# A mixture-of-experts stage on one core: expert rows are gated at evacuation and added into the result table by an indirect DMA

## What is computed

```python
h = rmsnorm(x2) * g_ffn
lg = h @ w_rg + b_rg;  grp = argmax(lg);  gate1 = softmax(lg)[grp]
top_v, top_i = top_k(expert logits within grp, 2)
gates = gate1 * softmax(top_v)                   # two gates per token
y[t]  = sum over the token's two experts e of
        gates[t, e] * ((silu(h[t] @ w_g[e]) * (h[t] @ w_u[e])) @ w_d[e])
out   = rmsnorm(x2 + y) * g_final
```

## Time and profile before

| | |
|---|---|
| median of 3 runs | 2068.12 us (2067.97 to 2071.73) |
| the profiled execution's own time | 2068.49 us |
| its span, first to last instruction | 2066.7 us |
| PE busy | 1762.6 us (85%) |
| DVE busy | 509.8 us (25%) |
| ACT busy | 325.3 us (16%) |
| POOL busy | 287.2 us (14%) |
| HBM read, written | 517.52 MB, 30.91 MB |
| q1, the DMAs issued by SP | 513.81 MB, 66.0% of 16 engines' span |
| q0, the DMAs issued by POOL | 19.17 MB, 3.2% |

### The profile page before, as it was taken

One profiled execution on the slowest core, in us unless ns is written; L12 is line 12 of the kernel. 1 busy time (PEld: TensorE's weight loads), 2 busy tenths in 40 slices (PEclk: granted clock), 3 DMA queues, 4 the chain that ended last, 5 costly groups with the idle time before them and its releaser, 6 DMA issues.

```text
span 2066.7 us, 27101 instructions
## 1 busy us (share of the span) xinstructions
PE 1762.6 (85%) x10986; PEld 1238.5 (60%) x10987; DVE 509.8 (25%) x1090; ACT 325.3 (16%) x573; POOL 287.2 (14%) x225
## 2 busy tenths in 40 slices
PE   7999999999899999985887787778787888977880
PEld 6888888887578888873544444434444454544440
DVE  6410999535365200014000000000000000000006
ACT  4003111004623011111111110101010111101112
POOL 0681322215800000000000000000000000000000
PEclk9999999999999999997999999998999999999895
DMA  5264121336954223317999999999999597999995
GB/s 234 64 153 111 68 81 61 122 147 190 14 199 162 102 82 125 140 37 292 386 405 422 395 413 395 406 391 393 393 398 393 199 399 324 412 403 411 414 416 218
DMA packets 88821, 535.86 MB, mean 259 GB/s; under 512 B 28761, under 2 KB 37465, under 8 KB 43673
## 3 DMA queue, kind: packets, MB, share of 16 engines
q1 hardware_dynamic: 74528, 513.81, 66.0%
q0 software_dynamic: 8800, 19.17, 3.2%
q10 hardware_dynamic: 5440, 2.13, 0.6%
HBM read 517.52 MB, written 30.91 MB: 265 GB/s over the span
## 4 chain that ended last, share of the span: by engine, by line
PE 53%; DMA 38%; POOL 3%; DVE 3%; ACT 2%; issue 1%; SPq 0%; POOLq 0%; ACTq 0%; DVEq 0%
DMA arena<-w_up_in 36%; PE psum L533 35%; PE psum L807 11%; PE psum L823 2%; DMA arena<-y_rows 1%; PE psum L662 1%; PE psum L668 1%; PE psum L570 1%; PE psum L787 1%; DVE arena L1564 1%; PE psum L732 1%; DVE arena L1557 1%; DMA y_rows<-arena 0%; POOL arena L1040 0%; POOL arena L1043 0%
## 5 line engine op out<-in xcount | busy, mean ns | idle before, releaser
L533 PE MATMUL psum<-arena 128*128 128x260 f32 x3328 | 741.5, 386 | 18.0 <-ACT arena L845 13.1
L533 PEld LDWEIGHTS psum<-arena 128*128 128x128 f32 x3328 | 637.1, 192 | 118.5 <-issue 10.2
L807 PE MATMUL psum<-arena 128*64 128x256 f32 x4352 | 541.8, 408 | 177.3 <-DMA arena<-w_up_in 150.5
L807 PEld LDWEIGHTS psum<-arena 128*64 128x64 f32 x4352 | 331.3, 148 | 397.0 <-DMA arena<-w_up_in 174.2
L823 PE MATMUL psum<-arena 128*64 128x512 f32 x1088 | 255.0, 623 | 16.9 <-ACT arena L1003 16.1
L1550 DVE TENSOR_TENSOR arena<-arena,psum 128x256 f32<-128x256 f32 x34 | 14.3, 421 | 959.9 <-PE psum L807 959.9
L823 PEld LDWEIGHTS psum<-arena 128*64 128x64 f32 x1088 | 78.1, 143 | 171.9 <-issue 143.5
L1128 POOL DMA_INDIRECT y_rows<-arena x34 | 33.9, 996 | 986.3 <-ACT arena L1008 941.2
L1003 ACT ACTIVATE arena<-psum 128x256 f32<-128x256 f32 x34 | 13.1, 384 | 509.2 <-PE psum L813 509.2
L787 PEld LDWEIGHTS psum<-arena 64*128 64x128 f32 x560 | 64.8, 203 | 22.1 <-issue 22.1
L1008 ACT ACTIVATE arena<-psum 128x512 f32<-128x512 f32 x68 | 36.9, 594 | 261.2 <-PE psum L823 261.2
(11 more groups left out here) (294 smaller groups left out, 1076.1 us busy)
## 6 DMA issues: line engine op xcount, KB each, us to landing
arena<-w_down_in SPq DMA_DIRECT2D x64, 2048.0 KB, 26.1
arena<-w_gate_in SPq DMA_DIRECT2D x64, 2048.0 KB, 28.1
arena<-w_up_in SPq DMA_DIRECT2D x64, 2048.0 KB, 27.7
arena<-w_in_in SPq DMA_DIRECT2D x32, 1024.0 KB, 4.8
arena<-w_out_in SPq DMA_DIRECT2D x16, 1024.0 KB, 4.8
arena<-k_cache_in SPq DMA_DIRECT2D x8, 1024.0 KB, 6.8
arena<-v_cache_in SPq DMA_DIRECT2D x8, 1024.0 KB, 4.8
arena<-y_rows SPq DMA_DIRECT2D x8, 1024.0 KB, 8.1
```

Source lines behind the costliest of these rows:

```text
L533: last = mm(pair(n)[:, h, :], w(kk), rhs(kk)[:, HALF * h:HALF * (h + 1)], start=(kk == begin), stop=(kk == kn - 1 and stop))
L807: last = mm(ps[64 * h:64 * h + 64, i // 2, 0:256], xtr[:, kk, :], w[:, kk, 256 * h:256 * (h + 1)], start=(kk == 0), stop=(kk == 15))
```

## The change

The table `y_rows` gives way to `y_sum`, with two rows of 1024 values per token, which is x2's shape. `store_x2` stores each group of x2 columns a second time, into `y_sum`. The scatter adds to its destination rows (`compute_op=ALU.add`). Since it adds, the rows have to carry their gate: each block needs its 128 gates as a column (`gate_now`), which comes from a one-hot product on PE with f32 operands, made once in block 0, and ACT multiplies by it in the evacuation. The order of a token's two experts (`swap`) no longer matters, and with it fall its DVE steps, one half of the list product, and in the tail the early loads and both gated additions. The tail loads `y_sum` after the last scatter into the weights' buffers and goes on to the norm. POOL waits for the second stores of x2 (`s_yst`) after its first two gathers.

The diff, cut to its core (declarations of buffers and semaphores are left out):

```diff
@@ SP @@
             def store_x2(g):
...
                 sp.dma_start(x2_rows[SEQ:T, c], x2_of[4][0:NS, c]).then_inc(s_x2st, 16)
+                c = slice(512 * g, 512 * (g + 1))
+                sp.dma_start(sums[0:SEQ, c].rearrange("(i p) n -> p i n", p=P), x2row[:, 0:4, c]).then_inc(s_yst, 16)
+                sp.dma_start(sums[SEQ:T, c], x2_of[4][0:NS, c]).then_inc(s_yst, 16)
...
-            last_base = sp.value_load(base_i[0:1, NE - 1:NE], min_val=1, max_val=NBLK)
-            sp.wait_ge(s_sct, last_base * 16)
...
-            load_y(f_low, 0, 4, s_flow)
-            sp.wait_ge(s_gdone, more + NE)
-            for i in range(4):
-                load_y(f_low, 0, i, s_flow)
             sp.wait_ge(s_ddone, more + NE)
             sp.dma_start(fg, t["g_final"].to_broadcast([P, DM])).then_inc(s_gf, 16)
             sp.wait_ge(s_sct, more * 16 + 16 * NE)
             for i in (4, 0, 1, 2, 3):
-                load_y(f_high, 1, i, s_fhigh[i])
+                sp.dma_start(fx[i][0:TOKS[i]], sums[P * i:P * i + TOKS[i], :]).then_inc(s_frow[i], 16)
@@ PE @@
-                last = mm(ps[:, 4, 0:2 * NBLK].rearrange("p (v b) -> p v b", v=2), lo16[:, c, :], hv16[:, c],
-                          start=(c == 0), stop=(c == 9))
+                last = mm(ps[:, 4, 0:NBLK], lo16[:, c, :], hv16[:, c, :], start=(c == 0), stop=(c == 9))
...
+                if first(n):
+                    pe.wait_ge(s_gate, 1)
+                    for c in range(10):
+                        last = mm(ps[:, 7, 0:NBLK], lo32[:, c, :], gate_b[:, c, :], start=(c == 0), stop=(c == 9))
+                    last.then_inc(s_gp, 1)
                 turn_rows(n + 1)
@@ ACT @@
+                act.wait_ge(s_is, n + 1)
                 act.wait_ge(s_ddone, n + 1)
                 for b in range(2):
-                    A(yrow[:, 512 * b:512 * (b + 1)], ps[:, 5 + b, :], ACT.Copy).then_inc(s_yv, 1)
+                    A(yrow[:, 512 * b:512 * (b + 1)], ps[:, 5 + b, :], ACT.Copy, scale=gate_now[:, j:j + 1]
+                      ).then_inc(s_yv, 1)
...
-                act.wait_ge(s_fin, c + 1)
+                act.wait_ge(s_frow[i], 16)
@@ POOL @@
                 pool.indirect_dma_start(
-                    out=y_rows, out_offset=bass.IndirectOffsetOnAxis(ap=idx_now[:, 2 + j:3 + j], axis=0),
+                    out=y_sum, out_offset=bass.IndirectOffsetOnAxis(ap=idx_now[:, 2 + j:3 + j], axis=0),
                     in_=yrow, in_offset=None,
-                    bounds_check=4 * T - 1, oob_is_err=False).then_inc(s_sct, 16)
+                    bounds_check=2 * T - 1, oob_is_err=False, compute_op=ALU.add).then_inc(s_sct, 16)
...
+            pool.wait_ge(s_yst, 16 * 8)
             blocks(pool, expert)
@@ DVE @@
-            tt(hv16[:, :, 0, :], wide_b, over(id_, NBLK), ALU.mult)
-            tt(hv16[:, :, 1, :], wide_b, over(tok1, NBLK), ALU.mult).then_inc(s_hot, 1)
+            tt(hv16, wide_b, over(tok1, NBLK), ALU.mult).then_inc(s_hot, 1)
...
-            for g in (first_gate, second_gate):
-                link(tt(g[:, :, 1:2], g[:, :, 0:1], swap.unsqueeze(2), ALU.mult))
-                link(tt(g[:, :, 0:1], g[:, :, 0:1], g[:, :, 1:2], ALU.subtract))
-            tt(gate_w[:, :, 0:1], first_gate[:, :, 0:1], second_gate[:, :, 1:2], ALU.add)
-            link(tt(gate_w[:, :, 1:2], first_gate[:, :, 1:2], second_gate[:, :, 0:1], ALU.add))
+            tt(lo32, iota_s.unsqueeze(1).to_broadcast([P, 10, P]), over(w_, P), ALU.is_equal)
+            tt(gate_b, wide_b, over(gate_w, NBLK), ALU.mult).then_inc(s_gate, 1)
...
+                if first(n):
+                    dve.wait_ge(s_gp, 1)
+                    link(dve.tensor_copy(gate_of, ps[:, 7, 0:NBLK]))
+                dve.tensor_copy(idx_now[:, 2 + j:3 + j], idx_s[:, bass.ds(n, 1)])
+                dve.tensor_copy(gate_now[:, j:j + 1], gate_of[:, bass.ds(n, 1)]).then_inc(s_is, 1)
...
-            for i, n in enumerate(TOKS):
-                stt(fx[i][0:n, 0:DM], f_low[i][0:n], gate_w[0:n, i, 0:1], fx[i][0:n, 0:DM], ALU.mult, ALU.add
-                    ).then_inc(s_fadd, 1)
...
-                stt(fx[i][0:n, 0:DM], f_high[i][0:n], gate_w[0:n, i, 1:2], fx[i][0:n, 0:DM], ALU.mult, ALU.add
-                    ).then_inc(s_fin, 1)
```

More of the change, by code:

```diff
@@ L243, in build @@
         s_z0 = sem("spare_scales_zeroed")
-        s_fin, s_fq, s_frt, s_fo = sem("final_loaded"), sem("final_sumsq"), sem("final_root"), sem("final_ready")
+        s_fq, s_frt, s_fo = sem("final_sumsq"), sem("final_root"), sem("final_ready")
         s_fst = sem("final_stored")
-        s_flow = sem("low_rows_loaded")
-        s_fhigh = [sem(f"high_rows_loaded{j}") for j in range(5)]
-        s_fadd = sem("low_rows_added")
+        s_frow = [sem(f"final_rows_loaded{j}") for j in range(5)]
+        s_yst, s_gp, s_gate = sem("sums_started"), sem("slot_gates_psum"), sem("slot_gates_ready")
         s_held = sem("pool_waited")
@@ L271, in build @@
         keep = Cols(ms + 4 * XW + DM // 2)
-        gate_w = keep(10).rearrange("p (t j) -> p t j", t=5)
+        gate_w = keep(10)
         idx_g = keep(NBLK + 2).bitcast(U32)
@@ L275, in build @@
         idx_now = keep(4).bitcast(U32)
-        none = keep(2 * NBLK)
+        none = keep(NBLK)
         gtab = keep(16)
@@ L284, in build @@
         assert keep.at <= at["W"], keep.at
+        lo32 = keep(10 * P).rearrange("p (c s) -> p c s", c=10)
+        gate_of = keep(NBLK)
+        gate_now = keep(2)
+        assert keep.at <= at["W"], keep.at
         rt = Cols(ea + 2 * XW)
         lo16 = rt(5 * P).bitcast(F16).rearrange("p (c s) -> p c s", c=10)
-        hv16 = rt(10 * NBLK).bitcast(F16).rearrange("p (c v b) -> p c v b", c=10, v=2)
+        hv16 = rt(5 * NBLK).bitcast(F16).rearrange("p (c b) -> p c b", c=10)
         in_group, elow, rest, elow2, rank = (rt(160).rearrange("p (t e) -> p t e", t=5) for _ in range(5))
@@ L296, in build @@
         late = Cols(at["V"] + 512 + XW)
-        chosen, swap = late(10), late(5)
-        C10 = [late(10) for _ in range(6)]
+        chosen = late(10)
+        C10 = [late(10) for _ in range(5)]
+        wide_b, gate_b = (late(10 * NBLK).rearrange("p (c b) -> p c b", b=NBLK) for _ in range(2))
         gmax, gidx, gsum, gate1, m1, m2, ex, ex_sum, gate_1st = (late(5) for _ in range(9))
         gexp = late(20).rearrange("p (t g) -> p t g", t=5)
-        first_gate, second_gate = (late(10).rearrange("p (t j) -> p t j", t=5) for _ in range(2))
         cnt, more_of, upto, base = (late(NE) for _ in range(4))
@@ L311, in build @@
         yjc = [ps[:, 2 * b, :].rearrange("p (j c) -> p j c", j=CHUNK) for b in range(2)]
[L312 to L316, removed]
+        fx = [view(at["W"] + DM * i, DM) for i in range(5)]
+        fg, fjunk = view(at["W"] + 5 * DM, DM), view(at["W"] + 6 * DM, DM)
         fstat = stat[:, 0:10].rearrange("p (s n) -> p s n", s=2)
@@ L1014, in _ @@
                 n = TOKS[i]
-                act.wait_ge(s_fin, c + 1)
-                A(fjunk[0:n], fx[i][0:n, 0:DM], ACT.Square, accum_out=fstat[0:n, 0, i:i + 1]).then_inc(s_fq, 1)
+                act.wait_ge(s_frow[i], 16)
+                A(fjunk[0:n], fx[i][0:n], ACT.Square, accum_out=fstat[0:n, 0, i:i + 1]).then_inc(s_fq, 1)
                 act.wait_ge(s_fq, c + 1)
@@ L1453, in _ @@
             tt(m16, hot1, hot2, ALU.add).then_inc(s_rb, 1)
-            p_, b_, w_, o_, id_, tok1 = C10
-            link(tt(swap, e1, e2, ALU.is_gt))
-            ts(id_[:, 0:5], tok, 2.0, 1.0, ALU.mult, ALU.add)
-            link(ts(id_[:, 5:10], tok, 2.0, 2.0, ALU.mult, ALU.add))
-            tt(id_[:, 0:5], id_[:, 0:5], swap, ALU.add)
-            tt(id_[:, 5:10], id_[:, 5:10], swap, ALU.subtract)
+            p_, b_, w_, o_, tok1 = C10
             ts(tok1[:, 0:5], tok, 1.0, None, ALU.add)
@@ L1498, in _ @@
             link(tt(wide_b, iota_b.unsqueeze(1).to_broadcast([P, 10, NBLK]), over(o_, NBLK), ALU.is_equal))
[L1499 to L1500 removed]
+            tt(hv16, wide_b, over(tok1, NBLK), ALU.mult).then_inc(s_hot, 1)
             dve.wait_ge(s_lst, 1)
[L1503 to L1507 removed]
+            src = ps[:, 4, 0:NBLK]
+            link(ts(none, src, 0.0, BIG, ALU.is_equal, ALU.mult))
+            stt(idx_g[:, 0:NBLK], src, -1.0, none, ALU.add, ALU.add)
+            link(stt(none, src, 2.0, none, ALU.mult, ALU.add))
             for j in range(2):
                 dve.tensor_copy(idx_now[0:CAP, j:j + 1], idx_g[0:CAP, j:j + 1]).then_inc(s_ig, 1)
[L1510 removed]
+            link(ts(idx_s, none, half_of, None, ALU.add))
             link(tt(ahead, upto.unsqueeze(1).to_broadcast([P, NBLK, NE]),
```

39 lines of the change are left out of this document (9 added, 30 removed).

## The result

The changed kernel takes 2078.72 us (median of 12 runs) against 2067.86 us before: ratio 1.0054, 95% interval 1.0043 to 1.0066, slower by 11 us. The prediction was 2077 us, slower. One of the 12 runs, at 2582.72 us with a lower granted clock, is left out of the ratio. The profiled execution is timed at 2082.76 us, that of before at 2068.49: the profiles differ by 14.3 us, 3.4 us more than the medians do, and that much is no part of the change.

A forecast was written before the change was run, and what follows sets the result against it. Engine time on the 16 DMA engines was taken to bound the block stage. Head +3, addition +21.9 and tail -16 sum to +9 us on the median 2068.12: 2077 us, range 2052 to 2103.

The forecast's parts named there:

- The addition: Block stage: each added read holds a DMA engine for a second row, 0.173 us on 2024 rows, +21.9 us.
- gathered row's price: Block stage, upper bound of the addition: engine held 0.27 us per added read, as for a gathered row, +34.2 us.
- Rival B: Scatters in the block stage: the added read runs beside the write, queue share unchanged, 2055 us; chance 0.23.
- rival D: Scatters: row-by-row addition, engine stands through read latency, at most +329 us, share far above 10%; chance 0.12.
- The landing: Block stage: a scatter's landing, 11 us at the median, could double without making the successor's evacuation wait; 0.
- The three early stores: Output projections: second stores of x2 with g = 0, 1, 2 are covered by PE; 0, else 4.6 us each.
- The head: Router to first gather: router 1.1 us shorter, gather meets weight chunks pushed back by the fourth store; +3 us.
- Gates: Block 0: ten gate products, 3.0 us on PE, delay the down chunks but queued weight loads cover it; 0.
- The tail: Last scatter to end: early loads and gated additions gone, end at 2050.5 against 2066.7, -16 us.
- The sum: Whole kernel: +3 + 21.9 - 16 = +9 us, put on the median 2068.12: 2077 us.
- A: Block stage, the forecast's own case: the added read holds the engine, 2077 us, own range 2072 to 2095; chance 0.52.
- ACT's evacuation: Block evacuation on ACT: the same instruction with a scale operand added, 0.

The follow-up runs named there:

- e1: The changed kernel with a plain scatter that overwrites the table's rows, the addition left out: 2050.94 us, ratio 0.9925 to the kernel before.
- e8: The kernel before with its own tables, tail and gates, only its scatter made to add, onto a table first filled with x2: 2097.44 us, ratio 1.0157.
- e9: The changed kernel with a block's rows spread over the partitions instead of packed on the first ones: 2057.26 us, ratio 0.9953 to the kernel before.
- e10: The changed kernel with a plain scatter (addition left out) and a block's rows spread over the partitions: 2034.80 us, ratio 0.9856 to the kernel before.
- e4: The changed kernel with the fourth second store of x2 issued behind expert 0's first weight chunks: 2078.63 us, ratio 1.0054 to the kernel before.
- e5: The changed kernel with a plain scatter, without the second stores of x2 and POOL's wait for them: 2051.11 us, ratio 0.9910 to the kernel before.
- e3: The changed kernel without the ten gate products on PE, gates a constant 0.5: 2076.73 us, ratio 1.0052 to the kernel before.
- e11: The kernel before with a block's rows spread over the partitions instead of packed on the first ones: 2051.68 us, ratio 0.9932.
- e12: The kernel before with rows spread over the partitions and DVE adding each low tile as it lands: 2051.92 us, ratio 0.9943.
- e6: The kernel before with a semaphore per low tile, so DVE adds each when it lands instead of after all five: 2061.24 us, ratio 0.9980.
- e7: As e6, but DVE stops after two low tiles until GpSimd has issued the last scatter: 2062.15 us, ratio 0.9980 to the kernel before.

## Why the prediction was right

**What bounds the kernel.** It was read rightly: engine time on the DMA engines is what the block stage costs. e1 takes the second reads away and e8 adds them, and each time the queue's share accounts for most of what the time moved by, with a few us left over; between e9 and e10, with the rows spread, it accounts for all (20.0 us, by the share 21.8).

**The addition, +21.9 us.** The choice between no cost, one row price and the gathered row's price fell on one row price, 0.173 us; the page gives 21.3 x 16 / 2080 = 0.164 us a row, give or take 0.016 for the rounding of the two shares. By the rule of the Trainium skill (Collectives: The Full Stack, Part 3: Why 7× under link rate), two source reads on one read ring halve the rate. The trace agrees with the half, 0.164 us on top of 0.173; that a ring is the reason no view shows. This is a mean beside weight loads: an adding row without them holds its engine for 0.51 us (last section), 0.34 more than a plain one, which at 2024 rows would be 43 us, outside the forecast's bounds. The reason given, that the engine is held for a second row like the first, so holds in the mean under load and not for the row alone. Rival B (the read beside the write) would have left the share at 5.4%, and rival D (a stall for each row) would have put it above 10. In total time the addition costs 26.7 us with 4.5 either way, in which the landing of the last scatter is 1.8; the forecast held that landing in the tail's sum.

**The landing, 0.** The scatters land in 12.6 us at the median and 14.0 at most, from 11.0 and 12.8. In both profiles every wait of ACT's evacuation ended with PE and none with a scatter.

**The three early stores, 0.** SP takes 1.8 us to issue one pair instead of the 0.8 taken, 1.4 of it for the small part. The router starts at 924.30 us in the changed kernel and at 925.93 before, so nothing of it shows.

**The head, +3 us.** In the profile it is 2.2 us net, from a router shorter by 1.5 us (1.1 forecast) and a gather that lands 3.8 us later (4.2 forecast). Block 0's first product comes at 956.4 us and not at the 958 to 959 given as a sign, for the router itself began 1.6 us earlier in this execution. In total time the head isn't resolved (e4, e5).

**Gates, 0.** The delay behind it is 4.0 us, not 3.0: the products took 2.36 us, and the down product that follows them 8.69 us instead of 7.1. In the windows under e3 the granted clock is 0.82, 0.50 and 0.83 from 976 us on, after the ten small products; half speed is the lower of its two levels, 1.2 GHz. Before, in e3 and in the other runs without these products the down product took 7.09 us, in those with them 8.6 to 8.8. e3 doesn't show that the delay costs time.

**The tail, -16 us.** It is -17.4 us. The last adding scatter's rows could be loaded 4.8 us after its start instead of the 6 taken, and the rest (2.5 + 3.6 + 5 x 2.5 + 4.35) came as worked out: 2.7 + 3.6 + 12.5 + 4.4.

**The sum.** +9 was forecast and +10.9 measured. What the forecast had not seen is that a mean over the engines isn't the whole price: the term of +21.9 was taken from it, while the place of the rows on the partitions is worth 14 to 21 us (e9, e11). That rows on neighbouring partitions load the engines unevenly is the reading that foretold this gain; no view shows the engines apart. Without its 1.8 us of landing the addition cost 24.9 us where 21.9 was forecast; the tail's extra gain of 1.4 and the head's 0.8 go the other way. That the sum came within 2 us is in part luck: the three misses, +3.0, -1.4 and -0.8 us, cancel in part, and the addition's own cost is known to 4.5 us only. Two bounds of the forecast were also added up short: with the head's +7.8 and the tail's -9, A ends at 2101 us and not at 2095, and B begins at 2051, just below the range's 2052. The result touches neither. In the two profiles the stage from the first reloaded chunk to the last scatter grew by 31.1 us (1059.7 to 1090.8), nearly 10 more than the queue's 21.3; e3 and e4, whose block stage is that of the changed kernel, have 1080.7 and 1086.7, so a part of the 10 is that one execution.

**ACT's evacuation** was priced at 0 as the same instruction. It is longer, 683 ns against 594 with the scale operand, and hidden as forecast. The Trainium skill (ScalarE: Activation LUTs, What ACT_TABLE_LOAD costs) gives 93 ns for each per-partition operand; the trace's 89 agrees.

## What to carry to other kernels

Where the DMA engines are the bound, an adding DMA saves no traffic: here it moves the second read from a tail, where the engines have room, to the stage in which they have none. Price it at twice the engine time of a plain one, and read that from the queue's share of engine time, since the bytes don't show it. And look at where the rows of an indirect DMA lie: with few valid rows, spread over the partitions instead of packed on the first ones, the kernel before gains 0.7% (e11, 2051.68 us, with e12's 2051.92 the fastest here that compute the whole result), and the changed one 1%, so that e9 beats the kernel before as well.

## What the runs showed of the hardware

- Valid rows packed on the first partitions cost more than the mean engine time of their gathers and scatters says: 14 us of 2065 in the kernel before (e11), of which the queue's share (3.2 to 3.1% of the span) has some 3.
- An adding row costs more when the engines have nothing else to do. The last scatter of the changed kernel, 56 rows, from 2053 to 2059 us, and that of e1, without the addition, from 2018 to 2024 us:

```profile
...
q0 software_dynamic: 144, 0.23, 30.0%
...
q0 software_dynamic: 144, 0.23, 10.5%
```

SP's queue is busy in these windows too, with `g_final` before the rows and the loads of y after them; from 2055 to 2057 us, when the adding rows run, it has 0.1% at most. Here 30.0% of 6 us on 16 engines is 28.8 us, 0.51 us a row, against 0.173 for a plain row in the same place and about 0.34, an estimate for the mean of all adding rows (0.173 + 0.164). e3, e4 and e9 repeat it with 29.2 to 30.6%. What the engine waits for, and that other queues' transfers fill part of that wait, is argued and was not tested.
- GpSimd's instruction for an adding scatter takes 1.55 us, for a plain one 1.00 us. That is hidden here but for the last scatter, where it is part of the 1.8 us.
- DVE's f32 additions of two SBUF operands hold up a GpSimd indirect DMA that is issued beside them (e6: 8.21 us; e7: 1.47 us), and its rows land 2 us later. The Trainium skill (SBUF — State Buffer, SBUF: two separate sides) tells in its box of an fp32 copy that locks GpSimd out of a shared port, and in its list of operations with two SBUF inputs, against a GpSimd operation that reads SBUF; e6 agrees with the second, at 8.21 us for 1.47. GpSimd's instruction began beside DVE's second addition of five and ended only after the fifth.
